# A two-block transformer layer on one core: four waits of TensorE and two column sums rearranged

## The reference

```python
# first block
h = rmsnorm(x, norm_mix_g)
a_val, a_gate, u_pool, c_x, c_b, c_c, g = split(h @ w_in)
a = causal_dwconv(a_val * sigmoid(a_gate), conv_a_w) + conv_a_b      # 31 taps, 512 channels
a = silu(layernorm(a, ln_a_g, ln_a_b)) @ w_a_out
c = (c_b * causal_dwconv(c_c * c_x, conv_c_w)) @ w_c_out
merged = gates[0] * a + gates[1] * pooled + gates[2] * c
x = x + merged @ w_o
x = x + memory_cross_attention(rmsnorm(x), rmsnorm(mem), w_xq, w_xkv, w_xo)
x = rmsnorm(x + mixture_of_16_experts(rmsnorm(x)))
# second block, two layers: a sparse attention (i = 0), then a differential one (i = 1)
mod = silu(c) @ w_ada[i] + b_ada[i]          # 6 modulation vectors of 1024
x = x + g1 * mixer_i(rms_norm(x) * (1 + sc1) + sh1)
x = x + g2 * (relu(h @ w_mlp_in[i]) ** 2 @ w_mlp_out[i])             # h: the same with sc2, sh2
```

## Time and profile before

| | |
|---|---|
| runs | 1307.42, 1305.44, 1308.18 us (median 1307.42) |
| profiled execution, its own time | 1306.28 us |
| its span | 1304.6 us, 24436 instructions |
| TensorE busy | 1280.9 us, 98% |
| VectorE, ScalarE, GpSimd busy | 948.8 (73%), 655.1 (50%), 94.5 us (7%) |
| granted TensorE clock, mean | 0.998 of full speed |
| DMA | 259.65 MB, mean 199 GB/s |

### The profile page before, as it was taken

How to read it: one execution, slowest core, us unless ns; L and a number is a source line. 1 busy time by engine, 2 the same in 40 slices (tenths; PEclk the granted TensorE clock), 3 DMA queues, 4 the chain that set the end, 5 groups by cost and what they waited for, 6 DMA issues and landing times.

```text
span 1304.6 us, 24436 instructions
## 1 busy us (share of the span) xinstructions
PE 1280.9 (98%) x10542; PEld 1228.8 (94%) x10542; DVE 948.8 (73%) x1199; ACT 655.1 (50%) x870; POOL 94.5 (7%) x140
## 2 busy tenths in 40 slices
PE   8999999999999999999999999999999999999998
PEld 7999999999899999999988689999999888999998
DVE  5779897764987677676876978887789676854443
ACT  5534445554643434344556747445456365654551
POOL 4021000001010000021000000100000010000000
PEclk9999999999999999999999999999999999999999
DMA  9765545545588777776623056999874432455550
GB/s 287 231 210 182 174 156 192 185 130 186 177 310 289 257 259 270 277 266 189 193 98 97 2 203 221 320 313 320 317 235 158 154 98 70 162 188 194 185 171 33
DMA packets 172700, 259.65 MB, mean 199 GB/s; under 512 B 5157, under 2 KB 147794, under 8 KB 172594
## 3 DMA queue, kind: packets, MB, share of 16 engines
q1 hardware_dynamic: 160906, 203.13, 47.0%
q0 software_dynamic: 10848, 53.69, 11.6%
q10 hardware_dynamic: 840, 1.28, 0.3%
HBM read 257.03 MB, written 1.05 MB: 198 GB/s over the span
## 4 chain that ended last, share of the span: by engine, by line
PE 85%; DVE 9%; ACT 3%; issue 2%; DMA 1%; SPq 0%; POOL 0%; DVEq 0%; ACTq 0%
PE ring L690 58%; PE acc L690 25%; DVE w_lo L2111 2%; ACT w_hi L1551 2%; PE acc L1326 1%; ACT h_hi L1551 1%; DVE arena L2151 1%; PE ring L1134 1%; ACT arena L1551 1%; DMA arena<-in_w_ada_dram 1%; DVE arena L2532 0%; DVE h_lo L2147 0%; DMA arena<-in_x_dram 0%; DVE norm L2126 0%; DVE arena L2352 0%
## 5 line engine op out<-in xcount | busy, mean ns | idle before, releaser
L690 PE MATMUL ring<-h_hi,w_hi 128*128 128x256 f32 (+1 forms) x2016 | 573.9, 285 | 4.5 <-DVE h_lo L2145 1.7
L690 PE MATMUL ring<-h_hi,w_lo 128*128 128x256 f32 (+1 forms) x2016 | 568.4, 282 | 0.0
L690 PE MATMUL ring<-h_lo,w_hi 128*128 128x256 f32 (+1 forms) x2016 | 566.4, 281 | 0.0
L2111 DVE TENSOR_TENSOR w_lo<-raw,w_hi 128x2048 fp32r<-128x2048 f32 (+1 forms) x188 | 429.3, 2290 | 160.7 <-ACT w_hi L1551 160.1
L1551 ACT ACTIVATE w_hi<-raw 128x2048 fp32r<-128x2048 f32 x192 | 363.3, 1896 | 129.9 <-PE ring L690 64.2
L690 PEld LDWEIGHTS ring<-h_hi,w_hi 128*128 128x128 f32 x2016 | 379.7, 188 | 10.5 <-issue 7.0
L690 PEld LDWEIGHTS ring<-h_lo,w_hi 128*128 128x128 f32 x2016 | 380.8, 189 | 2.4 <-issue 2.2
L690 PEld LDWEIGHTS ring<-h_hi,w_lo 128*128 128x128 f32 x2016 | 380.9, 189 | 0.0
L690 PE MATMUL acc<-e_hi,w_hi 128*128 128x256 f32 x768 | 216.8, 282 | 2.9 <-DVE e_lo L2820 1.5
L690 PE MATMUL acc<-e_lo,w_hi 128*128 128x256 f32 x768 | 214.9, 280 | 0.0
L690 PE MATMUL acc<-e_hi,w_lo 128*128 128x256 f32 x768 | 214.9, 280 | 0.0
(11 more groups left out here) (325 smaller groups left out, 1332.9 us busy)
## 6 DMA issues: line engine op xcount, KB each, us to landing
arena<-in_w_ada_dram POOLq DMA_DIRECT2D x64, 768.0 KB, 6.3
raw<-in_w_mlp_in_dram SPq DMA_DIRECT2D x32, 1024.0 KB, 5.4
raw<-in_w_mlp_out_dram SPq DMA_DIRECT2D x32, 1024.0 KB, 5.0
raw<-in_w_in_dram SPq DMA_DIRECT2D x24, 1024.0 KB, 6.1
raw<-in_w_e_gate_dram SPq DMA_DIRECT2D x16, 1024.0 KB, 5.7
raw<-in_w_e_up_dram SPq DMA_DIRECT2D x16, 1024.0 KB, 5.5
raw<-in_w_e_down_dram SPq DMA_DIRECT2D x16, 1024.0 KB, 4.9
raw<-in_diff_w_in_dram SPq DMA_DIRECT2D x12, 1024.0 KB, 5.2
```

The costliest lines, as they stand in the source:

```text
L690: return nc.tensor.matmul(dst, lhs, rhs, start=start, stop=stop, **kw)
L2111: tt(w_lo[q % RAW][:, 0:n], raw[q % RAW][:, 0:n], w_hi[q % SPL][:, 0:n].bitcast(F32), ALU.subtract)\
```

## The change

GpSimd adds the layer norm's four blocks to one before TensorE sums them: 512 columns plus 512, then 256 plus 256, once for the values (into the convolution's padded input, which is free by then) and once for their squares (in place). TensorE makes one product with ones for each instead of four. These two products move from behind x_v panels 0 and 1 into the middle of panels 1 and 2, whose two halves (one bank half each) are now issued apart. Memory's remainders move ahead of tap 17. The last pair of squares is summed after block k = 5 instead of k = 3 for "x" and "m1"; "ffn" and "m0" keep k = 3. In both MLPs `chunk_lo(1)` stands directly behind `ahead(PN[name] + 1)`; in layer 0 that is ahead of modulation piece 4, in layer 1 the order stays as it was. The DMAs stay the same in number, size and queue.

```diff
@@ shared semaphores: "folded" also for the layer norm's sums
-                  "folded": (2, ("x", "ffn", "m1")), ...
+                  "folded": (2, ("ln", "lv", "x", "ffn", "m1")), ...

@@ GpSimd, ahead of fold("x")
+            pool.wait_ge(S("conv_done"), 1)
+            nc.gpsimd.tensor_tensor(blk(A_PAD, 2), blk(SIG, 2), blk(SIG + 2, 2), ALU.add).then_inc(S("ln_folded"), 1)
+            pool.wait_ge(*sig("ln_folded", 1))
+            nc.gpsimd.tensor_tensor(blk(A_PAD), blk(A_PAD), blk(A_PAD + 1), ALU.add).then_inc(S("ln_folded"), 1)
+            pool.wait_ge(S("conv_squared"), 1)
+            nc.gpsimd.tensor_tensor(blk(CX, 2), blk(CX, 2), blk(CX + 2, 2), ALU.add).then_inc(S("lv_folded"), 1)
+            pool.wait_ge(*sig("lv_folded", 1))
+            nc.gpsimd.tensor_tensor(blk(CX), blk(CX), blk(CX + 1), ALU.add).then_inc(S("lv_folded"), 1)
             fold("x")

@@ TensorE: stats() goes, folded_sum() comes
+            def folded_sum(tag, src):
+
+                f = FL[tag + "_stat"]
+                open_fill(f)
+                pe.wait_ge(*sig(tag + "_folded", 2))
+                mm(bank(f)[:, 0:T], ones[:], src, True, True).then_inc(S(tag + "_summed"), 1)
+
-            def stats(tag, src, sem, n=KB):
-
-                f = FL[tag + "_stat"]
-                open_fill(f)
-                for k in range(n):
-                    if n < KB and k == 0:
-                        pe.wait_ge(S(sem), 1)
-                    ...
-                    last = mm(bank(f)[:, 0:T], ones[:], src(k), k == 0, k == n - 1)
-                last.then_inc(S(tag + "_summed"), 1)

@@ TensorE: the four x_v panels
             for i in range(4):
-                linear_rows(PN["x_v"] + i, x_v_fill(i))
-                if i == 0:
-                    stats("ln", lambda k: blk(SIG, 4)[:, k], "conv_done", n=4)
+                linear_rows(PN["x_v"] + i, x_v_fill(i), only=(0,))
                 if i == 1:
-                    stats("lv", lambda k: blk(CX, 4)[:, k], "conv_squared", n=4)
+                    folded_sum("ln", blk(A_PAD)[:, 0])
+                if i == 2:
+                    folded_sum("lv", blk(CX)[:, 0])
+                linear_rows(PN["x_v"] + i, x_v_fill(i), only=(1,))

@@ TensorE, x_panel(0): the last pair of squares is summed behind k = 5
-                (raw_next if i else raw_first)("x", PN["x_q"] + i, half_bank(x_q_fill(i)), *(() if i else ({3: (3,)},)))
+                (raw_next if i else raw_first)("x", PN["x_q"] + i, half_bank(x_q_fill(i)), *(() if i else ({5: (3,)},)))

@@ TensorE, mlp(l): the same for l = 1
-                raw_first(f"m{l}", PN[name], lambda b: acc[b], {3: (3,)})
+                raw_first(f"m{l}", PN[name], lambda b: acc[b], {(3, 5)[l]: (3,)})

@@ VectorE, the causal convolution
-            for tap in range(LOOP_TRIPS * per_turn):
+            for tap in range(LOOP_TRIPS * per_turn - 1):
                 add_tap(tap)
                 r, j = divmod(tap, per_turn)
-                if j in (1, 2, 4, 5) and tap < LOOP_TRIPS * per_turn - 1:
+                if j in (1, 2, 4, 5):
                     ahead(PN["gates"] + 4 * r + (1, 2, 4, 5).index(j) + 1)
             lows(blk(MEM_T, 8), h_hi, h_lo, "mem_hi", "mem_ready")
             ahead(PN["x_k"])
-            for i, tap in enumerate(range(LOOP_TRIPS * per_turn, TAPS_A - 1)):
+            for i, tap in enumerate(range(LOOP_TRIPS * per_turn - 1, TAPS_A - 1)):

@@ VectorE, mlp(l)
                 ahead(PN[name] + 1)
+                chunk_lo(1)
                 if l == 0:
                     ada(1, 4)
-                chunk_lo(1)
                 ahead(PN[name] + 2)
```

More of the change, by code:

```diff
@@ L278, in program @@
                   "exp": (1, ("group", "expert", "cmp", "lam")), "silu": (1, ("moe", "cmp")), "inverse": (1, ("n", "d", "s")),
-                  "folded": (2, ("x", "ffn", "m1")), "probs": (16, ("n", "d")), "scored": (16, ("n", "d")), "max": (16, ("n", "d")), "o_done": (8, ("n", "d")),
+                  "folded": (2, ("ln", "lv", "x", "ffn", "m1")), "probs": (16, ("n", "d")), "scored": (16, ("n", "d")), "max": (16, ("n", "d")), "o_done": (8, ("n", "d")),
                   "input_used": (KB - 1, ("gates", "x", "ffn", "moe", "m0", "d", "m1"))}
@@ L900, in stat_front @@
                     mm(bank(f)[:, 0:T], ones[:], sq[:, k], False, False)
-            def stats(tag, src, sem, n=KB):
-                f = FL[tag + "_stat"]
-                open_fill(f)
-                for k in range(n):
-                    if n < KB and k == 0:
-                        pe.wait_ge(S(sem), 1)
-                    elif n == KB and k % 2 == 0:
-                        pe.wait_ge(*sig(sem, k // 2 + 1))
-                    last = mm(bank(f)[:, 0:T], ones[:], src(k), k == 0, k == n - 1)
-                last.then_inc(S(tag + "_summed"), 1)
             pe.wait_ge(S("ident_landed"), 16)
```

## The result

The changed kernel takes 1310.51 us (median of 8 runs, 1309.55 to 1312.74), the kernel before 1307.09 (8 runs beside them, 1305.44 to 1308.18). The ratio is 1.0028, 95% interval 1.0019 to 1.0037: slower by 3.4 us, clear of noise, where 2 us faster was forecast. The profiled execution has a span of 1308.4 us against 1304.6, a difference of 3.8, and a mean granted clock of 0.994 against 0.998. I compare these two traces stage by stage, by the start of the same product in each; a lead is how many microseconds earlier the changed kernel starts it.

A forecast was written before the change was run, and what follows sets the result against it. TensorE's queue, 85% of the chain of waits, was taken as the bound. Terms -0.2 + 0.84 + 0.7 + 0.1 = 1.44, say 1.5 us, gave 1304.8 from the profiled execution or 1305.9 from the median; predicted 1305.3, range 1302.2 to 1308.0.

The forecast's parts named there:

- Part 1: First x_k panel: memory's remainders ahead of tap 17 remove TensorE's wait, gain 1.5 us; conv_done comes 1.6 later.
- Part 2: x_v stage: two folded sums replace eight products, gain 2.3 us, against three new waits of 1.4, 1.5 and 1.2.
- (a): Before the first folded sum: TensorE waits 1.4 us for GpSimd's adds.
- (b): Before x_v panel 2: TensorE waits 1.5 us for VectorE's remainder of that panel.
- (c): Second sum, middle of x_v panel 2: TensorE waits 1.2 us as GpSimd's adds take turns with VectorE's remainders.
- Stage: First x_k panel through x_v: net -0.3 us, taken as -0.2; bounds from +1.0 to -3.7.
- Part 3: x's last squares: later sum finds them ready, no wait, gain 0.84 us; bounds 0.4 to 0.9.
- Part 4: m1's last squares: gain 0.7 us, a new wait of 0.75 at the second chunk; bounds 0.5 to 1.45.
- Part 5: mlp0: second chunk's remainder ahead of piece 4 gains 1.69 us there, 0.1 net after piece 7; bounds +0.5 to -1.3.
- rival B: mlp0's start: modulation pieces bound it, new waits as counted or longer; gain 0.1 us, 1306.7, no change; chance 0.2.
- Rival A: x_v stage: the squares' folding is hidden, GpSimd gets in without turns; gain 2.7 us, 1304.1; chance 0.2.
- Rival C: x_v stage: GpSimd loses every turn at the squares, TensorE waits 4.7 us; slower, 1308.5 to 1309.9; chance 0.1.

The follow-up runs named there:

- the kernel with the early remainder: Changed kernel with raw request held until piece 7 landed, sums unfolded, x_v panel 2's remainder ahead of the first sum's wait: 1305.29 against 1307.09, ratio 0.9995.
- that with the early eviction: Changed kernel with raw request held until piece 7 landed, folds kept, ScalarE emptying x_v panel 0's bank before the centred values: 1305.18 against 1307.41, ratio 0.9991.
- both holds: Changed kernel, one raw panel request held until chunk 2's remainder is made (1305.27, ratio 0.9998) or until piece 7 has landed (1304.87, 0.9991), against 1306.02.
- part 5 alone: Kernel before with only the second chunk's remainder moved ahead of modulation piece 4: 1312.38 against 1306.02, ratio 1.0037.
- 11 runs and 5: Wide products placed between the compressed scores' halves: in the kernel before 1306.10 against 1307.38 (11 runs), in the best combined kernel 1300.79 (5 runs).
- without the folds: Changed kernel, raw request held until piece 7 landed, unfolded sums in the later places, early panel 2 remainder and panel 0 eviction: 1303.17 against 1307.41, ratio 0.9970.
- the late transposes: Changed kernel with the transposes that wait for piece 7 put behind chunk 2's down product on TensorE: 1308.12 against 1307.41, ratio 1.0007.

## Why the prediction was wrong, by its steps

**Part 1** (forecast 1.5): 1.55 at the first x_k product, 1.59 within its panel. Right; conv_done came 1.6 later from the same start, as said.

**Part 2.** (a) forecast 1.4, measured 1.37: right. (b) forecast 1.5, measured 1.54: right in size, wrong in cause. The prediction named VectorE's remainder; the wait ended with ScalarE's eviction, 0.3 us after the remainder was there. Two releasers within 0.5 us of each other, of which the trace of before showed neither as a wait; the kernel with the early remainder and that with the early eviction tell them apart. (c) forecast 1.2, measured 0.48: the turns of GpSimd and VectorE were there to the instruction (the second remainder ends 2.15 behind the first add, the second add 0.6 behind that remainder, as in the earlier trace rows), and GpSimd ended where it was forecast (196.09, which is 196.7 from before's start, against 196.9); TensorE came to it 0.5 later than forecast, because panel 2 had begun 0.4 later. Stage forecast -0.2, measured +0.15.

The turns are seen in the second add: 0.74 alone, 2.66 beside a remainder here. The Trainium skill, "SBUF — State Buffer", section "SBUF: two separate sides", has an exclusive lock of these two engines' port; by that rule, the trace agrees.

**Part 3** (0.84): 0.92, no wait at x's sum. Right where it stands. That the clock at 700 us takes about as much back was in no step: the prediction read "9 or more in all 40 slices" from the page and took one clock level for the whole. One slice of 33 us hides a fall to 0.7 for 5 us.

**Part 4** (0.7, new wait 0.75): 0.68, new wait 0.60. Right.

**Part 5** is the step that failed. Forecast: the next raw transfer "runs beside piece 7's", a delay of 0.4 and a gain of 0.1, at the worst 1.8 and -1.3. Measured: 1.7 at the part's own wait, as forecast, and -5.14 net. The two request times stood in the text, piece 7 at 814.98 and the raw panel moved from 816.45 to 814.7, and it was not noticed that this puts the raw panel ahead. The reason given against rival B was misread too: the 4.6 us of piece 7 were not taken "while the last 1 MB was still under way", for that panel, requested at 808.96, landed after 5.3 us, at 814.26, and piece 7 was requested at 814.98. Pieces of the same trace that did stand close behind a raw panel took 6.8 to 7.9 us. So the bound of even sharing was no bound: the request that went ahead took the engines for nearly its whole 1 MB, which is 2.8 us at the 371 GB/s that the profile gives for 816.5 to 818. Piece 7's way from issue to landing grew by 3.4 us (4.6 to 8.0). The second thing missed is that TensorE's idle time is not the end of the price: 2.0 us more went to the clock behind it. Rival B had the place and the sign but not the size; the range ended at 1308.0. Rival A fell, for the squares' sum did wait, with turns as in the earlier trace rows. Rival C, the only one that called for a slower kernel, fell as well: the wait it needed, 2.7 us or more at the middle of panel 2, was 0.48, so that its sign came out by another cause than its own.

The Trainium skill's "DMA: Bandwidth & Descriptors", section "Queues, rings and completion order", has each DMA engine go round, packet by packet, the queues that it has work for. Even sharing, for which the prediction took that rule, would have made the piece 1.8 late, and no run agrees with it: one packet of q0 beside 136 of q1 in 1.5 us. Whether q0 had packets ready in that time, which the rule asks for, no run here shows, so the rule itself is neither borne out nor refuted.

What is shown and what is not: that the order of the two requests makes the loss is shown by both holds, and by part 5 alone. Why the piece gets nothing while the raw panel moves (its descriptors written late, or fetched late behind the raw packets) was not tried apart. That parting the narrow products keeps the clock up rests on 11 runs and 5; kernels with them in one row also kept it in some runs, the kernel before in 34 of 98, so that something else has a share, and what it is stays open.

## What to carry to other kernels

When a change lets an engine release a buffer sooner, write down the order of all DMA requests around that moment, before and after; where two change places, count for the one behind the whole transfer ahead of it, not half (here 3.4 us for 1 MB). Holding back a request that had panels of slack cost nothing that these runs show. A wait can also cost time in the clock behind it: here waits of 4.1 and 4.5 us of TensorE cost another 1.5 and 2.0. And where an engine is paid for by another's help (sums folded by GpSimd), first ask whether the place of the work or its amount brought the gain: here the later places gave 1.6 us without the folds and 0.15 with them (with panel 2's remainder in its old place).

## What the runs showed of the hardware that was not expected

- A 768 KB transfer of GpSimd's queue requested 0.25 us behind a 1 MB transfer of SyncE's lands after 8.0 us, requested ahead of it after 4.4 to 4.6. Five others in the trace of before, requested less than 0.7 us behind such a panel, land after 6.8 to 7.9. From 818.5 to 823 in the changed kernel GpSimd's queue has 85.5% of the engines, and SyncE's, with the last 0.10 MB of its panel, 6.0%.
- Behind 4.5 us without work TensorE's granted clock was 0.61 over 6 us, behind 2.0 us (with the late transposes) 0.72 over the 6 us that hold the wait; behind 1.0 at the same place (raw request held) it stayed at 1.00.
- In a row of narrow products the clock fell in 12 of 15 traces while TensorE counted as busy throughout (5.00 of 5.00 us, clock 0.50): 7.05 us of them took up to 10.0. The kernel before ran in two groups of times 2.5 us apart, by mean clock 1.000 and 0.997.
